# Moving a row-fetched top-k block to the front of an expert stage, its rows into the residual's place, and its gate matmuls to bf16

## The reference

```python
s = jnp.einsum('thpd,hpkd->thpk', q, sub_keys).astype(jnp.float32)
s_top, i_top = lax.top_k(s, PEER_TOPK)
...
best_s, best_pos = lax.top_k(cand_s, PEER_TOPK)
experts = jnp.take_along_axis(cand_i, best_pos, axis=-1)
g = jax.nn.softmax(best_s, axis=-1)
act = jax.nn.gelu(jnp.einsum('thkd,td->thk', expert_u[experts], xb).astype(jnp.float32))
wgt = (g * act).astype(xb.dtype)
return jnp.einsum('thk,thkd->td', wgt, expert_v[experts])
```

## Time and profile before

| | before |
|---|---|
| time, median of 3 runs | 2530.11 us (2529.14 to 2533.96) |
| profiled execution, span from the first to the last instruction | 2531.0 us |
| PE / PEld busy | 2427.7 us (96%) / 2161.3 us (85%) |
| DVE busy | 1535.4 us (61%) |
| ACT / POOL busy | 939.2 us (37%) / 1213.8 us (48%) |
| DMA moved | 514.53 MB, mean 203 GB/s |

### The profile page before, as it was taken

How to read it: one execution, slowest core, us unless ns; L and a number is a source line. 1 busy time by engine, 2 the same in 40 slices (tenths; PEclk the granted TensorE clock), 3 DMA queues, 4 the chain that set the end, 5 groups by cost and what they waited for, 6 DMA issues and landing times.

```text
span 2531.0 us, 37403 instructions
## 1 busy us (share of the span) xinstructions
PE 2427.7 (96%) x12832; PEld 2161.3 (85%) x12832; DVE 1535.4 (61%) x2699; ACT 939.2 (37%) x1412; POOL 1213.8 (48%) x676
## 2 busy tenths in 40 slices
PE   7999998999999999978899989999999999999998
PEld 4878887899999999978888889998867888888887
DVE  5268343079979996769999999887246414422201
ACT  4463333244445554322333334333344323322222
POOL 3214443446678885555555554334411544444443
PEclk9999999999999999999999999999999999999999
DMA  7238333335555758999999999993311333223332
GB/s 278 67 121 294 134 98 93 99 116 176 176 161 198 267 208 308 362 354 399 399 399 399 400 400 380 360 342 112 94 41 42 113 95 100 89 94 99 96 96 75
DMA packets 254203, 514.53 MB, mean 203 GB/s; under 512 B 117728, under 2 KB 150880, under 8 KB 250016
## 3 DMA queue, kind: packets, MB, share of 16 engines
q1 hardware_dynamic: 197264, 345.82, 40.9%
q0 software_dynamic: 38416, 142.36, 14.2%
q10 hardware_dynamic: 18432, 25.17, 2.7%
HBM read 460.85 MB, written 52.43 MB: 203 GB/s over the span
## 4 chain that ended last, share of the span: by engine, by line
PE 65%; DVE 13%; DMA 8%; SPq 8%; issue 3%; ACT 1%; POOL 0%; DVEq 0%; ACTq 0%; POOLq 0%
PE bank L1240 16%; PE bank L1241 16%; PE bank L1242 16%; DMA GJ<-gate_dram 4%; PE pair L1240 4%; PE pair L1241 4%; PE pair L1242 4%; SPq L499 3%; DMA T<-in_u_rows,which 3%; SPq L582 2%; SPq L583 2%; PE pair L1563 2%; DVE T L2252 1%; DVE T L2129 1%; DVE T L2167 1%
## 5 line engine op out<-in xcount | busy, mean ns | idle before, releaser
L621 POOL TENSOR_TENSOR wlo<-wraw,whi 128x1024 fp32r<-128x1024 f32 x303 | 746.9, 2468 | 847.0 <-ACT whi L745 843.7
L1240 PE MATMUL bank<-HH,whi 128*128 128x512 f32 (+1 forms) x2048 | 747.3, 365 | 26.2 <-ACT actb L946 7.1
L1241 PE MATMUL bank<-HL,whi 128*128 128x512 f32 (+1 forms) x2048 | 742.5, 363 | 0.0
L1242 PE MATMUL bank<-HH,wlo 128*128 128x512 f32 (+1 forms) x2048 | 742.2, 362 | 0.0
L745 ACT ACTIVATE whi<-wraw 128x1024 fp32r<-128x1024 f32 x456 | 481.4, 1057 | 570.4 <-PE bank L1242 214.9
L1240 PEld LDWEIGHTS bank<-HH,whi 128*128 128x128 f32 x2048 | 385.7, 188 | 76.3 <-issue 24.1
L1242 PEld LDWEIGHTS bank<-HH,wlo 128*128 128x128 f32 x2048 | 385.5, 188 | 40.3
L1241 PEld LDWEIGHTS bank<-HL,whi 128*128 128x128 f32 x2048 | 385.7, 188 | 39.8 <-issue 0.5
L701 POOL DMA_INDIRECT VROW<-in_w,which x128 | 213.1, 1665 | 203.8 <-DVE YROW L2310 198.4
L1240 PE MATMUL bank<-WH,whi 128*128 128x384 f32 x512 | 181.0, 353 | 42.9 <-DVE WL L2287 42.9
L694 POOL DMA_INDIRECT T<-in_u_rows,which x128 | 145.5, 1137 | 158.1 <-DVE dots L2252 151.2
(11 more groups left out here) (411 smaller groups left out, 3650.7 us busy)
## 6 DMA issues: line engine op xcount, KB each, us to landing
wraw<-in_w SPq DMA_DIRECT2D x456, 512.0 KB
act_dram<-actb ACTq DMA_DIRECT2D x128, 192.0 KB
gate_dram<-GS SPq DMA_DIRECT2D x24, 1024.0 KB, 10.1
AJ<-act_dram SPq DMA_DIRECT2D x128, 192.0 KB
GJ<-gate_dram SPq DMA_DIRECT2D x128, 192.0 KB
adaw<-in_ada SPq DMA_DIRECT2D x32, 512.0 KB
ada<-in_ada SPq DMA_DIRECT2D x16, 512.0 KB, 13.9
NB<-in_nab POOLq DMA_DIRECT2D x4, 1024.0 KB
```

Of the source, the lines that this page charges most:

```text
L621: nc.gpsimd.tensor_tensor(wlo[:, slot, :, :].rearrange("p k c -> p (k c)"), wraw[:, slot, :, :].rearrange("p k c -> p (k c)"), whi[:, slot ...
L1240: pe.matmul(out_, ah, bh, start=first, stop=False, **kw)
L1241: pe.matmul(out_, ah, bl, start=False, stop=False, **kw)
L1242: return pe.matmul(out_, al, bh, start=False, stop=last, **kw)
```

## The change

Four things are done together.

1. DVE's top-k begins with the row-fetched block (`ORDER`), so its expert rows are known after one top-k instead of four. Scores, their evacuation and the exponentials follow that order; the softmax sum and division are made once for all blocks.
2. The fetched U rows go to the place of the residual `X`, which SP first saves to DRAM (`x_dram`, 2 MB) during the `wq` tiles and loads back early in the V stage. All 128 dots are made in the U stage: 12 in each of the last three top-ks, 72 among the 96 gate steps, 20 behind them. POOL issues the fetches between its `wlo` tiles. The V stage loses its 80 dots and their fetches.
3. The gate steps: indices, gates and one-hots are bf16. DVE makes both one-hots of a step in one instruction of 1024 elements (`indices_hot`) and the gates at their places in three bf16 parts in one of 1536 (`gates_hot`); TensorE makes 4 x 3 matmuls of 128 columns, which add up in PSUM; ACT copies the result. POOL's `offsets_j`, DVE's sum and the `window` copies to PSUM are gone. The gate steps begin after 68 tiles instead of 52.
4. POOL makes `wlo` for all U tiles up to the last, not DVE.

```diff
-U_LEAD = 3
-LEAD = 48
-GATE_IT = TB * U_LEAD + 1
+STEPS = SD // 4
+LEAD_IT = 16
+GATE_IT = LEAD_IT + 1
+ORDER = (TD, *range(TD))
+DOTS_TOP, DOTS_GATE = 12, 72
+FETCH_AT = 16
...
-        UROW = T[:, :, :].rearrange("p a b -> p (a b)").rearrange("p (n c) -> p n c", c=D)
+        UROW = X[:, :, :].rearrange("p a b -> p (a b)").rearrange("p (n c) -> p n c", c=D)
...
+            sp.wait_ge(tile_evac, G0["wq"])
+            sp.dma_start(x_dram[:, :, :], X[:, :, :]).then_inc(x_saved, 16)
...
+            with sp.Fori(0, 4) as i:
+                load_v(i)
+            sp.wait_ge(dot_done, P)
+            sp.dma_start(X[:, :, :], x_dram[:, :, :]).then_inc(x_back, 16)
...
+            for t in range(FETCH_AT, P):
+                lo(G0["U"] + t, t % R)
+                if t < gate0:
+                    due = R + min((t - FETCH_AT) * 3 * DOTS_TOP // (4 * LEAD_IT - FETCH_AT), 3 * DOTS_TOP)
+                else:
+                    due = R + 3 * DOTS_TOP + min(t + 1 - gate0, 4 * U_GATE) * DOTS_GATE // (4 * U_GATE)
+                for k in range(fetched, min(due, P)):
+                    fetch_u(k)
+                fetched = max(fetched, min(due, P))
+            for k in range(fetched, P):
                 fetch_u(k)
...
                 for e in range(4):
-                    t = 4 * half + e
-                    mm = pe.matmul(bank[4 + 2 * half + e // 2][:, e % 2 * 256:e % 2 * 256 + 256], OI[:, t, :],
-                                   OG[:, half, :, e, :], start=True, stop=True)
+                    for part in range(3):
+                        mm = pe.matmul(bank[4 + slot][:, e * P:(e + 1) * P], OH[:, slot, 0, :, e],
+                                       OG[:, slot % 2, part, :, e], start=(part == 0), stop=(part == 2))
...
+                def settled(ins, between=True):
+
+                    ins.then_inc(dve, 1)
+                    chain.add()
+                    turns[0] += between
+                    if n and between and turns[0] <= DOTS_TOP:
+                        dot()
+                    v.wait_ge(dve, chain.at())
...
+            def indices_hot(q):
+
+                if q >= 4:
+                    v.wait_ge(g_done, q - 3)
+                nc.vector.tensor_tensor(OH[:, q % 4, :, :, :], bc(iota4[:, :, :], 1, 2), bc(IJ[:, q, :, :], 2, P),
+                                        ALU.is_equal).then_inc(oh_ready, 1)
+
+            def gates_hot(q):
+
+                v.wait_ge(oh_ready, q + 1)
+                if q >= 2:
                     v.wait_ge(g_done, q - 1)
+                nc.vector.tensor_tensor(OG[:, q % 2, :, :, :], bc(OH[:, q % 4, 1, :, :], 1, 3), bc(G3[:, q, :, :], 2, P),
+                                        ALU.mult).then_inc(og_ready, 1)
+
+            indices_hot(0)
+            for q in range(STEPS):
+                if q + 1 < STEPS:
+                    indices_hot(q + 1)
+                gates_hot(q)
+                if (q + 1) * DOTS_GATE // STEPS > q * DOTS_GATE // STEPS:
+                    dot()
...
+            while dotted[0] < P:
+                dot()
```

More of the change, by code:

```diff
@@ L667, in _ @@
             pool.dma_start(keysT, A["keys"]).then_inc(keys_in, 16)
[L668 to L688, removed]
+            los(G0["wq"] + 3, G0["U"] + FETCH_AT - G0["wq"] - 3)
             def fetch_u(k):
@@ L1016, in _ @@
                 act_tile(124 + u, u, 16 * (62 + u // 2))
-            act.wait_ge(dot_done, LEAD)
-            nc.scalar.activation(acts[:, 0:LEAD], dots[:, 0:LEAD], ACT.Gelu_apprx_tanh).then_inc(dot_act, 1)
-            def v_tiles(i):
+            act.wait_ge(dot_done, P)
+            nc.scalar.activation(acts[:, :], dots[:, :], ACT.Gelu_apprx_tanh).then_inc(dot_act, 1)
+            load_roots()
+            with act.Fori(0, 31) as i:
                 for u in range(4):
@@ L1025, in v_tiles @@
                     pw_tile(i * 4 + (u + 3), (u + 3) % R)
-            def dots_act(i, half):
-                act.wait_ge(dot_done, i * 4 + (LEAD + 4))
-                ring = slice(LEAD + 4 * half, LEAD + 4 * half + 4)
-                nc.scalar.activation(acts[:, bass.ds(i * 4 + LEAD, 4)], dots[:, ring], ACT.Gelu_apprx_tanh).then_inc(dot_act, 1)
-            with act.Fori(0, (P - LEAD) // 8) as i:
-                for half in range(2):
-                    v_tiles(i * 2 + half)
-                    dots_act(i * 2 + half, half)
-            load_roots()
-            for j in range(P - LEAD, P - 3):
-                ahead(G0["V"] + j, 0)
-                pw_tile(j + 3, (j + 3) % R)
+            ahead(G0["V"] + 124, 0)
+            pw_tile(127, 127 % R)
             ahead(G0["V"] + 124, 1)
@@ new lines, in _ @@
+            for n in range(1, TB):
+                topk(n)
+            v.wait_ge(tk_exp, TB)
+            by_head = gsel[:, :, :].rearrange("p t (h k) -> p (t h) k", h=NH)
+            then(nc.vector.tensor_reduce(hs[:, 0, :], by_head, AX_X, ALU.add))
+            then(nc.vector.reciprocal(hs[:, 1, :], hs[:, 0, :]))
+            nc.vector.tensor_tensor(by_head, by_head, bc(hs[:, 1, :], 2, 16), ALU.mult).then_inc(tk_gate, 1)
+            v.wait_ge(gt_turned, 1)
+            nc.vector.tensor_copy(iota4[:, :, :], bc(iota[:, :], 2, 4))
@@ L2218, in g_sum @@
-            def g_sum(q, m):
-                v.wait_ge(g_high, q + 1)
-                t = 4 * (m % 16)
-                low = pair[m % 2][:, :, :].rearrange("p b (t w j) -> p w j (b t)", t=2, w=2)[:, 1]
-                g = GS[:, m // 16, :, t:t + 4]
-                nc.vector.tensor_tensor(g, low, g, ALU.add).then_inc(g_evac, 1)
-            def gate_blocks(i, first):
-                window(i, first)
-                for n in range(32):
-                    onehots(i * 32 + n, n, peeled=(first and n < 2))
-                    if n >= 2 or not first:
-                        g_sum(i * 32 + (n - 2), (n - 2) % 32)
@@ L2320, in v_steps @@
                     v_step(i * 4 + u, u, i)
[L2321 to L2332 removed]
+            v.wait_ge(dot_act, 1)
+            v_steps(0)
+            with v.Fori(1, 31) as i:
+                v_steps(i)
             expert_weights(31)
```

232 lines of the change are left out of this document (96 added, 136 removed).

## The result

The changed kernel takes 2626.4 us (median of 4 runs, 2624.7 to 2627.7) against 2532.0 for the kernel before (median of 4): ratio 1.037, 95% interval 1.035 to 1.038. The forecast was 2571 us with a range of 2493 to 2610: the direction was right, the size was not, and 2626 lies outside the range. The profiled execution spans 2625.9 us, 94.9 more than that of before.

A forecast was written before the change was run, and what follows sets the result against it. TensorE, 96% busy, was taken as the bound, with SBUF reads shared by DVE and POOL bounding the new gate steps. 2531.0 + 8 + 86 + 14 - 67 = 2572, set at 2571 us; range 2493 to 2610.

The forecast's parts named there:

- V (-67): V stage: without its 80 fetches and dots it runs at TensorE's full pace, 4.15 us a tile; -67 us.
- End of U (+14): Before V: last 16 fetches behind the last `wlo` leave TensorE idle 31 us; 33 lost instead of 19, +14 us.
- Gate steps (+86): 96 gate steps: SBUF reads shared by DVE and POOL's `wlo` raise a step from 2.55 to 3.45 us; +86 us.
- TensorE's 3.43: Gate steps: TensorE's time per step at the higher matmul price, 0.113 us each; the upper bound beside 2.76.
- The sign named for it: Gate steps: 96 steps in about 330 us with TensorE waiting for `OG` would show the forecast right.
- The lead (+8): U tiles before the first gate matmul: added dots delay DVE's top-ks, so TensorE waits some 8 to 11 us; +8 us.
- 36 x 0.61 x 1.2 = 26 us: Lead: 36 dots each lose half a `wlo` on average while POOL is 61% busy; 26 us of DVE time.
- The bound of +20: Lead: upper bound on the time it loses, beside the +8 us taken and the lower bound of 0.
- V gives nothing: Rival, V stage: something else holds V at its old pace, only its start gains 10 us; 2629 us, chance 0.05.

The follow-up runs named there:

- e2: Changed kernel with TensorE making only two of the three gate parts, eight matmuls a step instead of twelve; output lacks the third part: 2621.7 us, ratio 1.034.
- e1: Changed kernel with the token row that every dot multiplies with kept in PSUM instead of its SBUF copy: 2567.7 us, ratio 1.013.
- e6: Changed kernel with three of every four gate steps altered: contiguous weights, contiguous moving operand, or 64 weight columns; gates wrong, timing only: 2620.0 us, one run.
- e10: Changed kernel with dot row in PSUM, token-pair one-hots, two gate parts, last 16 fetches spread over the tail, 48 top-k dots: 2519.2 us, ratio 0.993.
- e9: Changed kernel with dot row in PSUM and one-hots laid out by token pairs (moving operand columns 4 bytes apart), all three parts: 2535.1 us, ratio 1.000.
- e12: e10 with 36 dots in the top-k instead of 48, and 72 in the gate steps; also lacks the third gate part: 2507.4 us, ratio 0.990.

## Why the prediction was wrong

- **V (-67): right.** 525.6 us for 126 tiles is 4.17 a tile, beside the 4.15 of the stretch that the forecast took it from.
- **End of U (+14): right in kind and size.** +12: one wait of 28.8 us for `actb`, where 31 were worked out, behind 16 fetches in 28.0 us.
- **Gate steps (+86): +92.** The forecast put the read path at 3.43 us and TensorE at 2.76, and named TensorE's 3.43 as upper bound. DVE's prices (0.60 and 0.87 per instruction, by bytes) hold, and the read path measured alone is 3.45 (e2). But TensorE alone gives 3.51 (e1), so TensorE's 2.76 was wrong, and that the term still came out is in part luck: two bounds lie at one place. The sign named for it, TensorE waiting for `OG`, is missing: TensorE is busy for all 337.2 us. Its price was near the row chosen as upper bound, for a reason not considered: the stride of the moving operand, not the weights (e6). What the float32 row itself pays for was not measured. 1024 bf16 elements start their successor 0.60 us later, as 512 of float32 do; so the rule cited from the Trainium skill, "VectorE: DVE Perf Modes", § The perf-mode tier table, agrees with the trace.
- **The lead (+8): the step that failed; +57.** The forecast let each of 36 dots lose half a `wlo` in 61% of cases, "36 x 0.61 x 1.2 = 26 us". Measured, a dot lost 2925 - 1211 = 1.7 us, 62 us in all: 36 more than that. 9 more came from `babf` (8 x 1.17), 7 from the instruction of 64 elements (4 x 1.85), 6 from the first row (12.1 us in place of 6). That is 58. Against it the rest of the top-ks took some 9 us less than before, 4 of them in a cast that was no longer caught, and the 3 us put down for the division were already in the 204. What is left is the 46 us by which DVE was late (844 for 798). Two assumptions were wrong. Contention was taken as a chance meeting, while POOL's next `wlo` stands behind a fetch that the dot's end releases (36 waits, one for each of the 36 dots), and so meets the next dot or an instruction of the top-k nearly every time; this is read from the rows, as in e10. And contention was taken as turns, one for one, as in the earlier trace rows, while a waiting DVE instruction can be passed by three `wlo`. The bound of +20 was given without a working of its own.
- **From DVE to TensorE.** DVE's lateness shows as one wait of 15.7 us for `gsel`, but TensorE's lead is 57.7 us longer than in e1, where it never waits. POOL's `wlo` came late behind fetches that waited for dots (16.4 us in the lead), ACT's gelu stood behind an exponential that waited for DVE (39.2 - 28.8 = 10.4), and the granted clock was 0.94 on average in place of 1.00, which is the other 15 us: TensorE was busy for 302.7 us with what takes it 287.4 in e1. The clock falls to its lower level, 1.2 GHz, where TensorE waits: from 830.0 to 846.5 us it was granted 0.55 on average, and TensorE was busy for 2.5 of those 16.5 us. The forecast counted one wait at the end and none along the way.
- **The rivals.** "V gives nothing" was nearest in time (2629) and wrong in its stage, which is luck. No rival had the lead as its place: contention there was a term with a mean and no tail, and so the range ended 16 us too low.

What is left open: why three `wlo` pass a waiting DVE instruction in some places and one in others. The runs show it, and none was made for it.

## What to carry to other kernels

When two engines share a path and one's next instruction is released by the other's last, do not price their contention as an average overlap. Follow the chain of releases and price every meeting in full, small instructions too. Or give one side an operand in PSUM, which here made 58 us vanish with one operand (e1). When a stage has two bounds, measure each with the other lifted; here one repair alone gave 0 us in the gate steps, the other alone 6, and both together 33. And look at the stride of a moving operand before counting matmuls.

## What the runs showed of the hardware

- A bf16 matmul of 128 columns starts the next one 0.056 us later when its moving operand's columns are 2 bytes apart (0.67 / 12, e6), 0.057 at 4 bytes (0.68 / 12, e9), 0.1125 at 8 (1.35 / 12). With the columns 8 bytes apart, contiguous weight columns give next to nothing (0.109), and 64 weight columns in place of 128 are dearer (0.128, both e6). The Trainium skill, "SBUF — State Buffer", § Door 1: The DMA port swizzle, says that one can stride for free up to 8 bf16 elements. For TensorE's moving operand the trace does not agree: four elements double the price.
- A DVE instruction that meets a `wlo` is held whatever its own size: one of 64 elements takes 2.07 us on average in place of 0.22. It can be held for three in a row: 7.29 us for a dot of 1.2. Some with a single input are held too: in e10 the cast of 256 elements takes 2.42 us in place of 0.29 and the copy of 2048 takes 2.86 in place of 1.29. The Trainium skill, "SBUF — State Buffer", § Who interferes with whom, names both kinds, instructions with two SBUF inputs and copies and casts in a mode that uses both ports, and the trace agrees that both are held.
- DVE takes an inner run of two bf16 elements at the same price as one of four: the shortest one-hots instruction stays at 0.68 us in e9, e10 and e12.
